# Reordered attention, block-wise modulation on two engines, and earlier evictions in a two-layer hybrid SSD, attention and Fourier kernel

## The reference, cut to what matters

```python
def trunk_layer(x, cvec, lw, ctx):
    sh1, sc1, g1, sh2, sc2, g2 = adaln_params(cvec, lw["w_ada"], lw["b_ada"])
    h = rms_norm(x, lw["g_pre_mix"]) * (1 + sc1) + sh1
    mix, ctx_out = token_mixing(h, lw, ctx)
    x = x + g1 * rms_norm(mix, lw["g_post_mix"])
    h = rms_norm(x, lw["g_pre_ffn"]) * (1 + sc2) + sh2
    x = x + g2 * rms_norm(conv_mlp(h, lw), lw["g_post_ffn"])
    return x, ctx_out
```

## Time and profile before

| | us |
|---|---|
| median of 3 runs | 2056.64 |
| profiled execution, its own time | 2050.58 |
| its span, first to last instruction | 2049.0 |
| PE busy | 1838.1 |
| DVE busy | 1108.3 |
| ACT busy | 877.4 |
| GpSimd busy | 34.8 |

### The profile page before, as it was taken

How to read it: one execution, slowest core, us unless ns; L and a number is a source line. 1 busy time by engine, 2 the same in 40 slices (tenths; PEclk the granted TensorE clock), 3 DMA queues, 4 the chain that set the end, 5 groups by cost and what they waited for, 6 DMA issues and landing times.

```text
span 2049.0 us, 32299 instructions
## 1 busy us (share of the span) xinstructions
PE 1838.1 (90%) x11178; PEld 1683.0 (82%) x11178; DVE 1108.3 (54%) x1817; ACT 877.4 (43%) x1516; POOL 34.8 (2%) x56
## 2 busy tenths in 40 slices
PE   4977999889999989999989788988899997999995
PEld 2965888668989789999969468976699996999995
DVE  3657454564334577367375665356543446764754
ACT  3543444563343454244354355346533334543432
POOL 1000000000000000000000000000000000000000
PEclk8989999999999999999999899999999999999998
DMA  7420323122343533433453103331143444333331
GB/s 297 154 75 22 105 101 124 42 82 101 124 154 123 214 115 123 154 125 127 150 199 128 44 2 129 128 108 48 55 137 114 164 154 175 125 121 124 123 114 62
DMA packets 56031, 244.08 MB, mean 119 GB/s; under 512 B 6336, under 2 KB 6416, under 8 KB 52336
## 3 DMA queue, kind: packets, MB, share of 16 engines
q1 hardware_dynamic: 49824, 181.43, 25.7%
q0 software_dynamic: 6096, 61.19, 7.7%
HBM read 238.63 MB, written 3.96 MB: 118 GB/s over the span
## 4 chain that ended last, share of the span: by engine, by line
PE 64%; issue 19%; DVE 10%; ACT 5%; DMA 1%; DVEq 0%; ACTq 0%; POOL 0%; POOLq 0%
PE ps L1189 18%; PE ps L1191 17%; PE ps L1190 17%; PE ps L569 3%; DMA region<-in_ada 1%; DVE rstd L1626 1%; PE ps L598 1%; ACT w_hi L1376 1%; PE ps L628 1%; ACT region L770 1%; PE ps L507 1%; PE ps L479 1%; DVE wide L1630 1%; PE ps L584 1%; PE ps L446 1%
## 5 line engine op out<-in xcount | busy, mean ns | idle before, releaser
L1376 ACT ACTIVATE w_hi<-raw 128x1024 fp32r<-128x1024 f32 x344 | 364.8, 1060 | 820.3 <-PE ps L1191 819.6
L1189 PE MATMUL ps<-h_hi,w_hi 128*128 128x384 f32 x1632 | 556.0, 341 | 21.3 <-DVE h_lo L1618 20.4
L1190 PE MATMUL ps<-h_lo,w_hi 128*128 128x384 f32 x1632 | 552.2, 338 | 0.0
L1191 PE MATMUL ps<-h_hi,w_lo 128*128 128x384 f32 x1632 | 552.0, 338 | 0.0
L1614 DVE TENSOR_TENSOR w_lo<-raw,w_hi 128x1024 fp32r<-128x1024 f32 x248 | 304.5, 1228 | 402.8 <-ACT w_hi L1376 368.4
L1189 PE MATMUL ps<-in_hi,w_hi 128*128 128x384 f32 x992 | 342.7, 345 | 33.4 <-DVE in_lo L842 10.6
L1191 PE MATMUL ps<-in_hi,w_lo 128*128 128x384 f32 x992 | 339.2, 342 | 0.0
L1190 PE MATMUL ps<-in_lo,w_hi 128*128 128x384 f32 x992 | 338.9, 342 | 0.0
L1189 PEld LDWEIGHTS ps<-h_hi,w_hi 128*128 128x128 f32 x1632 | 309.2, 189 | 25.9 <-issue 15.1
L1190 PEld LDWEIGHTS ps<-h_lo,w_hi 128*128 128x128 f32 x1632 | 309.6, 190 | 0.4 <-issue 0.3
L1191 PEld LDWEIGHTS ps<-h_hi,w_lo 128*128 128x128 f32 x1632 | 309.2, 189 | 0.0
(11 more groups left out here) (216 smaller groups left out, 1718.3 us busy)
## 6 DMA issues: line engine op xcount, KB each, us to landing
raw<-in_weights SPq DMA_DIRECT2D x346, 512.0 KB, 3.2
region<-in_ada POOLq DMA_DIRECT2D x20, 2048.0 KB, 9.5
wide<-in_ada POOLq DMA_DIRECT2D x2, 1536.0 KB, 7.4
region<-in_ada POOLq DMA_DIRECT2D x2, 1536.0 KB, 7.2
region<-in_state POOLq DMA_DIRECT2D x2, 1024.0 KB, 10.1
region<-in_ada POOLq DMA_DIRECT2D x4, 512.0 KB, 9.0
out_state<-wide POOLq DMA_DIRECT2D x4, 512.0 KB, 2.9
region<-in_consts POOLq DMA_DIRECT2D x2, 897.0 KB, 4.9
```

The costliest lines, as they stand in the source:

```text
L1189: pe.matmul(out, ah, bh, start=start, stop=False)
L1190: pe.matmul(out, ah, bl, start=False, stop=False)
L1191: m = pe.matmul(out, al, bh, start=False, stop=stop)
L1376: act.activation(w_hi[:, j % AHEAD, :], raw[:, nxt, :], ACT.Copy).then_inc(hi_made.sem, 1)
```

## The change

It makes these edits.

1. Attention. Tile 6 moves ahead of the scores of heads 0 and 1, tile 7 behind them. The wait for the values moves from ahead of the head loop to a place after the scores of head 2. The first fill tile moves ahead of turn 6 and waits for the exponentials of 7 heads; the second comes after the loop. ACT and DVE evict tile 0 of the second half at the last head of the first half, and tile 1 right after it, before the last `o_hi` and `o_lo`.
2. Merge stages: DVE evicts a product tile first and splits the weights after it. In z, f and w_o, ACT evicts ahead of `refill`; in z and w_o, DVE's use of the result comes ahead of `split`.
3. Modulation: `times_rstd` is interleaved with the blocks of `modulate`; the context columns of even blocks go to ACT. The two `vector` calls of `modulate` come ahead of the reciprocal and wait for all four columns.
4. Buffers: four side buffers at the start of a layer (the third in `region`, the fourth in `mix` and `ckv`), two `mod_rows`, two sets of columns. Sides 0 to 3 of the second layer are loaded during the first. Caches and states are loaded after side 3 has been used.
5. PE's order: side 3 goes between blocks 4 and 5 of the sum of norm 1; side 7 ahead of w_o; sides 8 and 9 and their columns ahead of norm 6; columns 11 ahead of the sum of norm 7.
6. End of a layer: the squares of norm 7 go to a ring of 4 buffers instead of `mix`; `vector(L, 5)` comes ahead of norm 7.

```diff
@@ attention, PE @@
+            tile(half, 6)
             pe.wait_ge(taken.sem, taken.at(L, t0 + 6 + AHEAD))
...
             scores(0)
             scores(1)
-            tile(half, 6)
             tile(half, 7)
-            pe.wait_ge(taken.sem, taken.at(L, t0 + 8 + AHEAD))
-            pe.wait_ge(v_ready.sem, v_ready.at(L, 2 * half + 2))
             for h in range(HALF):
                 if h + 2 < HALF:
                     scores(h + 2)
+                if h == 0:
+                    pe.wait_ge(taken.sem, taken.at(L, t0 + 8 + AHEAD))
+                    pe.wait_ge(v_ready.sem, v_ready.at(L, 2 * half + 2))
+                if h == HALF - 2:
+                    pe.wait_ge(exped.sem, exped.at(L, base + HALF - 1))
+                    fill[0]()
                 turn(h)
-                if h >= HALF - 2 and len(fill) > h - (HALF - 2):
-                    fill[h - (HALF - 2)]()
                 if h >= 2 and h % 2 == 0:
                     output(h // 2 - 1)
+            for tile_ in fill[1:]:
+                tile_()
             output(HALF // 2 - 1)
@@ attention, ACT (DVE likewise with take, maxima and o_lo) @@
-            for i in range(6):
-                evict(i)
+            for i in range(2 * half, 7):
+                evict(half, i)
             exponent(0)
-            evict(6)
             exponent(1)
-            evict(7)
+            evict(half, 7)
             for h in range(HALF):
                 out_turned(h)
                 if h + 2 < HALF:
                     exponent(h + 2)
+                if h == HALF - 1 and half == 0:
+                    evict(1, 0)
                 if h >= 3 and h % 2:
                     o_hi(L, base // 2 + h // 2 - 1)
+            if half == 0:
+                evict(1, 1)
             o_hi(L, base // 2 + HALF // 2 - 1)
@@ w_o, ACT @@
-                    refill(L, t, turn, j)
+                    act.wait_ge(used.sem, used.at(L, t + 1))
                     square(mix[:, k, :], ps[:, 2 * (j % 2), 0:T])
+                    refill(L, t, turn, j)
                     act.activation(wide[:, k, :], ps[:, 2 * (j % 2), 0:T], ACT.Copy)...
@@ start of a layer, PE @@
                 side(L, 0)
                 side(L, 1)
-                norm_sum(L, 1, wide)
+                pe.wait_ge(caches_free.sem, caches_free.at(L, 1))
                 columns(L, 0)
                 columns(L, 1)
                 side(L, 2)
-                side(L, 3)
                 columns(L, 2)
+                norm_sum(L, 1, wide, None, {5: lambda: side(L, 3)})
                 columns(L, 3)
@@ start of a layer, ACT @@
+                rows(L, 0)
+                rows(L, 1)
+                rows(L, 2)
                 for k in range(DB):
                     act.wait_ge(x_ready.sem, x_ready.at(L, k + 1))
                     square(wide[:, k, :], x[:, k, :])
-                rows(L, 0)
                 norm(L, 1, D)
-                rows(L, 1)
-                rows(L, 2)
                 rows(L, 3)
@@ start of a layer, DVE (the middle of a layer likewise) @@
-                norm(L, 1)
                 dve.wait_ge(params_in.sem, params_in.at(L, 16))
+                dve.wait_ge(cols_made.sem, cols_made.at(L, 4))
                 vector(L, 0)
-                for k in range(DB):
-                    times_rstd(L, k, x)
                 vector(L, 1)
                 after(dve).then_inc(cols_used.sem, 1)
+                norm(L, 1)
                 modulate(L, 0)
@@ modulate, DVE @@
+                times_rstd(L, 0, x)
                 for k in range(DB):
-                    dve.wait_ge(scaled_by.sem, scaled_by.at(L, 2 * which * DB + k + 1))
-                    dve.tensor_scalar(wide[:, k, 0:CTX], ...)
+                    if k + 1 < DB:
+                        times_rstd(L, k + 1, x)
+                    if k % 2:
+                        dve.wait_ge(scaled_by.sem, scaled_by.at(L, 2 * which * DB + k + 1))
+                        dve.tensor_scalar(wide[:, k, 0:CTX], ...)
                     if k >= 2:
                         lo(k - 2)
@@ middle of a layer, PE @@
                 side(L, 6)
+                side(L, 7)
                 project(L, "w_o", y_hi, y_lo, (y_lo_made, y_lo_made.at(L, 3 * DB + 1)))
                 columns(L, 6)
-                side(L, 7)
+                columns(L, 7)
                 added_sum(L, 1)
-                columns(L, 7)
                 side(L, 8)
+                side(L, 9)
+                columns(L, 8)
+                columns(L, 9)
                 norm_sum(L, 6, mix)
```

More of the change, by code:

```diff
@@ L1014, in attention_dve, with take @@
             t0 = STAGES[f"heads{half}"][0]
-            def take(i):
-                t = t0 + i
+            def take(half, i):
+                t = STAGES[f"heads{half}"][0] + i
                 b = head_bank(half, t)
@@ L1043, in take @@
                 split(L, t, t // RING, t % RING)
-            for i in range(6):
-                take(i)
+            for i in range(2 * half, 7):
+                take(half, i)
             base = half * HALF
@@ L1074, in attention_dve @@
             even(0)
-            take(6)
-            take(7)
+            take(half, 7)
             for h in range(HALF):
@@ L1364, in _ @@
                     m.then_inc(down_made.sem, 1)
-                norm_sum(L, 7, mix, DOWN_LAST[1])
+                pe.wait_ge(down_taken.sem, down_taken.at(L, DB // 2 + DOWN_LAST[1].index(4) + 1))
                 columns(L, 11)
+                for n in range(DB):
+                    pe.wait_ge(squares.sem, squares_at(L, 7, n + 1))
+                    pe.matmul(ps[:, 7, 0:T], ones, last_squares[n % 4], start=(n == 0), stop=(n == DB - 1))\
+                      .then_inc(last_summed.sem, 1)
         @block.scalar
@@ L1782, in z_tile @@
                     tick_taken()
+                    split(L, t, turn, j)
                     if k >= 2:
```

140 lines of the change are left out of this document (88 added, 52 removed).

## The result

The changed kernel takes 2021.91 us (median of 4 runs, 2018.73 to 2022.64), the kernel before 2056.86 us beside it. The ratio is 0.983, with a 95% interval of 0.9813 to 0.9847. The profiled execution took 2018.73 us, its span is 2017.0 us.

The account below looks back on a forecast made before the run. PE, busy 90% of the span, was taken as the bound, with its idle time and low-clock matmuls to win. Terms summed to -35.2 us from 2050.6, giving 2015.4, scaled to 2021.4 us; range 2010 to 2036.

Parts of the forecast that it names:

- Attention with its entrance: Attention: reordered tiles close PE's stops, 13 us a layer (bounds 9 and 15.5); entrance stop 0.4 us a layer shorter.
- five hand-worked stops: Attention: stops left before tile 6, turn 0, turn 1, second half's tile 3 and scores: 1.4, 1.9, 1.35, 1.1, 1.5 us.
- Start of layer 0: Layer 0's start: sum blocks, root, rows, columns, vectors and reciprocal stand behind side 3; +5 us, bounds +3.9 and +12.
- Start of layer 1: Layer 1's start: sum and reciprocal end later, but multiplications are interleaved; -1.3 us, bounds -3 and +4.
- Middle: Norms 5 and 6 to up0: earlier root, interleaved multiplications, vectors ahead of reciprocal; 4.0 us a layer, -8 in all.
- f: After the last f tile: the copy before the Fourier transforms no longer stands behind a refill; -0.96 us a layer.
- w_o: Before w_o: side 7 takes 1.85 us of the 2.07 us stop, 1.7 us from the clock; -2.0 us in all.
- (a): Attention gains only its longest stops, 9 us a layer, clock falling as often as before; 2029.5 us, chance 0.17.
- (b): Layer starts cost more: +11 us in layer 0 at half clock, +4 in layer 1; 2033 us, chance 0.13.
- (d): Attention's stops belong to something else, so moving tiles does nothing there; -9 us, 2047.5 us, chance 0.05.
- (e): Attention: short, evenly spread stops hold the clock at 1.2 GHz; slower, about 2078 us at 62 us a layer, chance 0.05.
- (c): All stops close and clock stays up: attention 15.5 us a layer, layer 0's start +3.9; 2015 us, chance 0.13.

Follow-up runs that it names:

- e1: The kernel before with only the changed attention of all three engines: 2022.46 us, ratio 0.9854.
- e7: The changed kernel, but loads of sides 2 and 3 wait for the use of sides 0 and 1, as before: 2025.33 us, ratio 0.9851.
- e6: The changed kernel with norm 1's sum whole ahead of side 3, the reciprocal under side 3, rows(2) behind the root: 2012.68 us, ratio 0.9779.
- e8: The changed kernel with all eight multiplications of a norm ahead of modulation's blocks again: 2024.29 us, ratio 0.983.
- e2: The changed kernel with the attention of before: 2052.0 us, ratio 0.9997.
- e10: The changed kernel with side 7 and its rows behind w_o again, columns 7 behind norm 5's sum: 2031.09 us, ratio 0.9895.

## Why the prediction was right

The time, 2021.4, is 0.5 us from the measured 2021.91. But the terms are not all right, and their errors cancel.

- **Attention with its entrance, -26.8 predicted, -32.7 in the profile.** The mechanism held: e1 shows that attention alone gives the change, as far as the measurement can tell. The five hand-worked stops measure 1.47, 1.70, 1.34, 1.65 and 1.46 us against 1.4, 1.9, 1.35, 1.1 and 1.5. Idle time is 15.3 and 13.1 us where about 13 was forecast; the 0.67 us before head 2's scores, once a half, are not in the sum. The term that was mis-sized is the clock. The twelve stages of the changed order are 15.5 us shorter on average than the four of the old one, and idle time makes 8.7 of it (25.4 to 16.7). The other 6.8 are busy time of the same matmuls, and the clock accounts for them: by the mean clocks of 0.921 and 0.966 a layer spent 22 us of attention at the low level and now spends 8.5, and each costs half. The prediction had 9.6 us less idle time and 13 in all, so 3.4 for the clock, though by its own working the 22 us at the low level had cost 11. It foresaw the stops of 1.9 and 1.35 us as the place where the clock would still fall, and there it fell in 19 of 32 halves.
- **Start of layer 0, +5 predicted, +6.8 to the end of the first tile.** The order of the steps behind side 3 was as worked out, and it is nearly all of the cost: e7, which issues the loads as before, has +5.9. Of the rest a part belongs to "I cost their earlier issue at nothing". The queue was never empty, but four loads issued at once share it with the weights: the second weight tile's rounding moved from 22.81 to 27.19, and with it the first `rows`. Side 3 in return landed earlier (35.3 us against 38.5 in e7). Over the profiles the early issue cost 0.2 to 3 us to the first matmul.
- **Start of layer 1, -1.3 predicted, -0.7 to the first matmul, +0.4 to the end of the first tile.** Within its bounds. e6 shows 2.3 us to be had there.
- **Middle, -8 predicted, -6.1.** The first matmul of up0 comes 3.9 us nearer to the end of w_o, where the text had 4.3 and, among its signs, about 5. From the first multiplication to the first matmul it takes 3.3 us instead of 6.6, where the text had 3.7 less. The step that was mis-sized is DVE's work behind the reciprocal, put at 8.9 us: from the first multiplication to the end of the last `h_lo` it took 10.2 us (12.3 before). So the last `h_lo` came 2.8 us sooner a layer instead of 3.6, and PE's end behind it moved by 0.5 us in one layer and by nothing in the other, instead of 1. Of what the interleaving gives to the first matmul (1.4 us by e8) only 0.9 us a layer is left when the tile is done.
- **f, -1.9 predicted, -0.4.** The stop itself fell from 1.52 to 0.58 us, the 0.94 of the text, in both layers. The stages from out_mla to out_fft are only 0.2 us shorter a layer in this profile and 1.4 shorter in that of e2 (184.45 against 185.89), because their matmuls stood 174.7 ns apart here in out_mla and f, and 173.3 before and in e2, at a granted clock of 1.00 in all three. With the spacing of before the 0.94 are there.
- **w_o, -2.0 predicted, -2.1.** The side fills the stop as worked out. The stop of 2.07 us was followed by the low level in 2 of the 4 places that have it (layer 0 before, layer 1 of e1), and with side 7 ahead of w_o the clock did not fall in any of 20. But the text costed sides 8 and 9 "at nothing" without saying that side 9's buffer must be free (e10).
- **Not foreseen: +3.5 us in the projection and ssd of layer 1.** That stage lasted between 278.9 and 284.5 us over the profiles, most of them with the same instructions in it, so one profile's 3.5 us are no sure effect of the change. A part is again the spacing of the matmuls, 176.5 to 176.7 ns in its long runs where the profile before had 173.8 to 174.6.

Rival (a) is refuted by the clock (0.97 over the twelve stages, where (a) had it falling as often as before), (b) by the starts (+7.2 in all, not +15), (d) by e1. Rival (e) is refuted: with stops of 1.2 to 1.7 us spread over the stage the clock was never under 0.94. (c) was nearest in attention, where its 15.5 us a layer are the mean of the profiles, but not for its reason: the clock did not stay up, and 13 to 15 us of idle time are left. The page "TensorE: Matmul & The Clock Gate" of the Trainium skill, section "A second HAM failure mode: psum-queue depth-cycling", would have made (e) the outcome. The clock does swing between its levels at the first heads here, but over the twelve stages that leaves a mean of 0.97, more than the 0.92 of before. The page "ScalarE: Activation LUTs", section "What ACT_TABLE_LOAD costs", would have added a drain to the switch; in e6 the load begins at 27.41 and the next activation at 28.70, 0.01 us after its 1.28 us, as in the earlier trace rows.

The total holds by luck in part. The starts came 3.5 us dearer than the sum had them, the middle gained 1.9 less, f 1.5 less, and the projection of layer 1 lost 3.5; against them stand attention with 5.9 more and the feed-forward with 1.9 that nobody forecast. The profile's -32.0 and the medians' -34.9 differ by the scatter of single executions; the sum said -35.2.

## What to carry to other kernels

Work out the stops of a hand-ordered stage one by one; the five that were worked out here came out within 0.6 us. But the sum of idle time is not the time: 6.8 of the 15.5 us gained in attention were busy time of the same matmuls, because the long stops after which the clock fell are gone. So close the longest stops first (2.7 us and more in this kernel), and don't judge an order by one profile. Before a side job is moved, follow its buffer to the next load that uses it: moving side 7 alone back cost 6.6 us a layer through side 9, which the diff hardly shows. And something that ends just before a reciprocal on the critical path (side 3, `vector`) can run beside it, as in e6, which is 9 us faster for it and for `rows(2)` behind the root.

## What the runs showed of the hardware that I had not expected

- The same instructions in the same order ran at different granted clocks: 0.946 to 1.000 in attention over 12 stages, with lengths from 125.2 to 129.2 us. A single profile can't price an order of work closer than that.
- The clock fell behind nearly every long stop (25 of 26 of 2.7 to 4.1 us) and behind hardly any single short one (2 of 68 of 1.4 to 2.0 us); stops close together stood between (19 of 32 halves). No run holds one stop at a chosen length, so this is a count over these kernels and no rule.
- At a granted clock of 1.00 the starts of matmuls of 384 columns lie 173.3, 174.7 or 176.6 ns apart, one value for tens of microseconds, and which one differs between stages and executions of the same work. What sets it stays open. The run of 528 matmuls through out_mla and f in layer 0, before and after (from the start of its first matmul to that of its last it is 91.34 and 92.06 us):

```profile
481.21:572.40 91.19, 91.19 (x528) 91.19 (x528) 35.14 (x38) 29.24 (x36) 0.00 (x0) 1.00 0.38 130
469.40:561.20 91.80, 91.80 (x527) 91.80 (x527) 35.15 (x38) 29.27 (x36) 0.00 (x0) 1.00 0.38 129
```

- The DMA engines at the start were busy 79% before and 72% after, for a stretch that was 5.6 us longer. Issuing more loads at once did not move the bytes sooner as a whole; it moved which of them came first (side 3 earlier, a weight tile 4.4 us later).
